# 48 instead of 40 tokens on fetched expert rows, with a fifth row block, six dot products moved into the gated units and three low parts moved to VectorE

## The reference

```
top_s, top_i = lax.top_k(s, PEER_TOPK)                       # per head and half key
best_s, best_pos = lax.top_k(cand_s, PEER_TOPK)
idx, gates = take_along_axis(cand_i, best_pos), softmax(best_s)
h   = gelu(einsum('chkd,cd->chk', peer_u[idx], x)) * gates   # 128 picks a token
out = einsum('chk,chkd->cd', h, peer_v[idx])
```

## Time and profile before

| | before |
|---|---|
| median of 3 runs | 968.71 us (968.62 to 969.97) |
| the profiled execution, its own time | 968.82 us |
| its span, first to last instruction | 967.0 us |
| busy: PE, PEld | 956.6 (99%), 918.7 (95%) us |
| busy: DVE, ACT, POOL | 741.6 (77%), 623.3 (64%), 589.8 (61%) us |
| granted TensorE clock over the span | 0.998 |

### The profile page before, as it was taken

The page is one execution under the profiler, slowest core; times in us unless marked ns, Lnnn a source line. Parts: engine busy times, 40 slices in busy tenths (PEclk is TensorE's granted clock), DMA queues, the critical chain, the costliest instruction groups (busy, mean ns, idle before and its releaser), DMA issues.

```text
span 967.0 us, 22095 instructions
## 1 busy us (share of the span) xinstructions
PE 956.6 (99%) x7344; PEld 918.7 (95%) x7344; DVE 741.6 (77%) x1606; ACT 623.3 (64%) x1227; POOL 589.8 (61%) x308
## 2 busy tenths in 40 slices
PE   9999999999999999999999999999999999999997
PEld 8998899999889999999999999999999999999996
DVE  7683673534756798888788888759888989898995
ACT  6773376555557666676899999865555555555553
POOL 4685624587425999989887888853434434343520
PEclk9999999999999999999999999999999999999999
DMA  7473313355654766666555456579999999999981
GB/s 263 143 235 125 131 48 110 110 175 187 224 181 152 233 221 215 215 215 215 188 177 182 175 195 217 197 277 395 338 370 340 362 356 348 357 343 356 354 296 44
DMA packets 64752, 223.96 MB, mean 232 GB/s; under 512 B 7964, under 2 KB 10012, under 8 KB 64573
## 3 DMA queue, kind: packets, MB, share of 16 engines
q1 hardware_dynamic: 52604, 180.54, 52.3%
q0 software_dynamic: 11520, 41.95, 12.3%
q10 hardware_dynamic: 576, 0.82, 0.2%
HBM read 221.28 MB, written 1.06 MB: 230 GB/s over the span
## 4 chain that ended last, share of the span: by engine, by line
PE 97%; DVE 1%; DMA 1%; ACT 0%; issue 0%; ACTq 0%; POOL 0%; DVEq 0%
PE PS L962 21%; PE PS L1034 20%; PE PS L966 12%; PE PS L1039 12%; PE PS L533 4%; PE PS L534 4%; PE PS L535 4%; PE PS L911 3%; PE PS L543 2%; PE PS L919 2%; PE PS L988 1%; PE PS L989 1%; PE PS L697 1%; PE PS L547 1%; PE PS L952 1%; PE PS L767 1%
## 5 line engine op out<-in xcount | busy, mean ns | idle before, releaser
L1566 POOL TENSOR_TENSOR lo<-raw,hi 128x1024 fp32r<-128x1024 f32 x191 | 456.9, 2410 | 143.3 <-ACT hi L1117 128.8
L1117 ACT CAST hi<-raw 128x1024 fp32r<-128x1024 f32 x203 | 212.6, 1048 | 48.8 <-DMA raw<-in_u_units 27.5
L962 PE MATMUL PS<-xb,hi 128*128 128x432 f32 x1024 | 225.1, 361 | 0.0
L1034 PE MATMUL PS<-xb,hi 128*128 128x432 f32 x1008 | 219.7, 359 | 0.0
L962 PEld LDWEIGHTS PS<-xb,hi 128*128 128x128 f32 x1024 | 182.8, 189 | 5.1
L1034 PEld LDWEIGHTS PS<-xb,hi 128*128 128x128 f32 x1008 | 179.7, 189 | 5.4
L2258 DVE TENSOR_TENSOR lo<-raw,hi 128x2048 fp32r<-128x2048 f32 x63 | 144.2, 2289 | 15.6 <-ACT hi L1456 12.2
L1456 ACT CAST hi<-raw 128x1024 fp32r<-128x1024 f32 x128 | 134.1, 1047 | 4.4 <-DMA raw<-in_v_units 4.3
L966 PEld LDWEIGHTS PS<-xb,lo 128*128 128x128 f32 x1024 | 133.6, 191 | 2.0 <-POOL lo L1566 0.6
L1039 PEld LDWEIGHTS PS<-xb,lo 128*128 128x128 f32 x1008 | 132.5, 191 | 2.8 <-DVE lo L2258 1.1
L1495 ACT CAST xb<-arena 128x216 fp32r (+1 forms) x126 | 47.0, 373 | 135.2 <-PE PS L1039 134.1
(11 more groups left out here) (361 smaller groups left out, 1536.1 us busy)
## 6 DMA issues: line engine op xcount, KB each, us to landing
raw<-in_u_units SPq DMA_DIRECT2D x128, 512.0 KB
raw<-in_v_units SPq DMA_DIRECT2D x128, 512.0 KB
raw<-in_w_in_units SPq DMA_DIRECT2D x43, 512.0 KB
raw<-in_w_q_units SPq DMA_DIRECT2D x16, 512.0 KB
raw<-in_w_proj_units SPq DMA_DIRECT2D x8, 512.0 KB
raw<-in_w_out_units SPq DMA_DIRECT2D x8, 512.0 KB
arena<-bias_rows SPq DMA_DIRECT2D x2, 512.0 KB, 4.8
arena<-in_subkeys_t SPq DMA_DIRECT2D x1, 1024.0 KB, 6.1
```

The costliest lines, as they stand in the source:

```text
L962: mm(o[:, 0:2 * TD].rearrange("p (s t) -> p s t", s=2), hi[:, w, P * k:P * k + P], xb[:, k, :, 0:TD], start=(k == 0), stop=False, skip_gro ...
L1034: return mm(PS[:, V_BANKS[c], 0:2 * TD].rearrange("p (s t) -> p s t", s=2), hi[:, (U_V + j) % 4, P * c:P * c + P], coef_slot(u + j)[:, :, ...
L1117: nc.scalar.copy(hi[:, j, :], raw[:, j, :]).then_inc(hi_made, 1)
L1566: nc.gpsimd.tensor_tensor(lo[:, w, :], raw[:, w, :], hi[:, w, :].bitcast(F32), ALU.subtract).then_inc(lo_pool, 1)
```

## The change

TG rises from 40 to 48 (GROUPS 32 and 16), so TD falls to 208, SECOND to 52, and there are 48 + 48 fetches instead of 40 + 40. A fifth row block is added (block 5 of the arena; SLOTS = 5). Eleven fetches instead of four are issued by GpSimd among the expert units, behind the low parts listed in GATHER_AT. Six dot products are done in the gated steps of EARLY_STEPS, behind the one-hots, and in every gated step the one-hots now come before second_halves and gated. The low parts of units 12, 28 and 44 are made by VectorE, behind expert_halves of the unit two before; GpSimd waits for each and passes the count on. Loops that held these steps are written out.

```diff
-GROUPS = [32, 8]
+GROUPS = [32, 16]
 TG = sum(GROUPS)
 TD = T - TG
 SECOND = TD // 4
...
-        rows_at = [area(P * TD + D * n, D) for n in range(4)]
+        rows_at = [area(P * TD + D * n, D) for n in ROW_BLOCKS]
...
+        rows_in = [sem(f"gathered_rows_in{n}") for n in range(SLOTS)]
...
-            LO_DVE_V = LO_FIRST + 2 * HEADS - LO_QUERY - (U_V + 2)
+            LO_DVE_V = LO_FIRST + 2 * HEADS - LO_QUERY + len(LO_BY_VECTOR) - (U_V + 2)
...
-            with pool.Fori(0, GATHER_AT) as i:
-                for j in range(4):
-                    make_lo(U_U, i, j)
-            pool.wait_ge(picks_in, PICKS_IN)
-            for g in range(4):
-                make_lo(U_U, GATHER_AT + g, 0)
-                gather(g)
-                for j in range(1, 4):
-                    make_lo(U_U, GATHER_AT + g, j)
-            with pool.Fori(GATHER_AT + 4, NKEYS // 4) as i:
-                for j in range(4):
-                    make_lo(U_U, i, j)
+                    out=rows_at[g % SLOTS], out_offset=None, in_=rows,
+                    in_offset=bass.IndirectOffsetOnAxis(ap=pick_row[:, n:n + 1], axis=0)).then_inc(rows_in[g % SLOTS], 16)
+
+            for u in range(NKEYS):
+                if u in LO_BY_VECTOR:
+                    pool.wait_ge(lo_dve, LO_FIRST + 2 * HEADS - LO_QUERY + LO_BY_VECTOR.index(u) + 1)
+                    pool.wait_ge(lo_pool, U_Q - LO_FIRST + LO_QUERY + u)
+                    pool.sem_inc(lo_pool, 1)
+                else:
+                    make_lo(U_U, u // 4, u % 4)
+                if u == GATHER_AT[0]:
+                    pool.wait_ge(picks_in, PICKS_IN)
+                if u in GATHER_AT:
+                    g = GATHER_AT.index(u)
+                    if g >= SLOTS:
+                        pool.wait_ge(rows_used, g + 1 - SLOTS)
+                    gather(g)
             make_lo(U_V, 0, 0)
             make_lo(U_V, 0, 1)
-            for g in range(4, 2 * GATHERS):
-                pool.wait_ge(rows_used, g - 3)
+            for g in range(len(GATHER_AT), 2 * GATHERS):
+                pool.wait_ge(rows_used, g + 1 - SLOTS)
                 gather(g)
...
                     columns_done[0] -= RANK_PER_UNIT
                     expert_halves(summed[0] // 4, summed[0] % 4)
+                    if summed[0] + 2 in LO_BY_VECTOR:
+                        make_lo(U_U, (summed[0] + 2) // 4, (summed[0] + 2) % 4)
                     summed[0] += 1
...
-                dve.wait_ge(rows_in[g % 4], 16 * (g // 4) + 16)
-                V.scalar_tensor_tensor(out=rows_at[g % 4], in0=rows_at[g % 4], scalar=1.0, in1=repeated[group], op0=ALU.mult,
+                dve.wait_ge(rows_in[g % SLOTS], 16 * (g // SLOTS) + 16)
+                V.scalar_tensor_tensor(out=rows_at[g % SLOTS], in0=rows_at[g % SLOTS], scalar=1.0, in1=repeated[group], op0=ALU.mult,
                                        op1=ALU.mult, accum_out=pick_dot[:, n:n + 1]).then_inc(rows_used, 1)
 
-            def gated_step(i, j):
-
-                gates_in(i, j)
+            def gated_step(i, j, early_dot=None):
+
+                n = 4 * i + j
+                if n < SECOND:
+                    gates_in(i, j)
+                if n + 2 < SECOND:
+                    one_hots(i, j + 2)
+                if early_dot is not None:
+                    dot(early_dot)
                 second_halves(i, j)
-                gated(i, j - 1, 4)
-                one_hots(i, j + 2)
+                gated(i, j - 1, min(4, SECOND + 3 - n))
...
             final = GATED_UNITS // 4 - 1
-            with dve.Fori(1, final - 1) as i:
-                for j in range(4):
-                    gated_step(i, j)
-            for j in range(4):
-                n = 4 * final - 4 + j
-                if n < SECOND:
-                    gates_in(final - 1, j)
-                second_halves(final - 1, j)
-                gated(final - 1, j - 1, min(4, SECOND + 3 - n))
-                if n + 2 < SECOND:
-                    one_hots(final - 1, j + 2)
+            for n in range(4, 4 * final):
+                if n == (EARLY_STEPS + [4 * final - 1])[0]:
+                    dve.wait_ge(picks_in, PICKS_IN)
+                gated_step(n // 4, n % 4, EARLY_STEPS.index(n) if n in EARLY_STEPS else None)
...
-            dve.wait_ge(picks_in, PICKS_IN)
-            g = 0
+            g = len(EARLY_STEPS)
             for q in range(1, NKEYS // 2):
                 value_operands(q // 4, q % 4)
                 while g < min(2 * GATHERS, ROWS_AFTER[q]):
@@ -2308,10 +2307,15 @@
...
-SPREAD_AT, GATHER_AT = 16, 26
+SPREAD_AT = 16
+LO_BY_VECTOR = [12, 28, 44]
+SLOTS, ROW_BLOCKS = 5, [0, 1, 2, 3, 5]
+EARLY_STEPS = [14, 19, 24, 29, 34, 39]
+GATHER_AT = [79, 84, 89, 94, 99, 104, 110, 112, 114, 116, 118]
 ROW_WORK = [(True, GROUPS[0] + n) for n in range(GROUPS[1])] + [(True, n) for n in range(GROUPS[0])]
 ROW_WORK += [(False, GROUPS[0] + n) for n in range(GROUPS[1])] + [(False, n) for n in range(GROUPS[0])]
-ROWS_AFTER = [len(ROW_WORK) * q // (NKEYS // 2 - 3) for q in range(NKEYS // 2)]
+EARLY = len(EARLY_STEPS)
+ROWS_AFTER = [EARLY + (len(ROW_WORK) - EARLY) * q // (NKEYS // 2 - 3) for q in range(NKEYS // 2)]
```

More of the change, by code:

```diff
@@ L304, in block_program @@
         act_evac = sem("act_evacuated")
-        dve_evac = sem("dve_evacuated")
         dve_step = sem("dve_step")
-        pe_step = sem("pe_step")
         act_step = sem("act_step")
@@ L359, in block_program @@
         staged_made, picks_in = sem("gathered_picks_staged"), sem("picks_and_rows_repeated")
-        rows_in = [sem(f"gathered_rows_in{n}") for n in range(4)]
+        rows_in = [sem(f"gathered_rows_in{n}") for n in range(SLOTS)]
         rows_used, dots_gelu, taker_made = sem("gathered_rows_used"), sem("gathered_dots_gelu"), sem("taker_made")
@@ L1478, in _ @@
             final = GATED_UNITS // 4 - 1
-            with act.Fori(1, final - 1) as i:
+            with act.Fori(1, final - 2) as i:
                 for j in range(4):
@@ L1483, in _ @@
                     low_one_hots(i, j + 1)
-            for j in range(4):
-                second_right_copy(final - 1, j)
-                second_half_gelu(final - 1, j - 1)
-                if 4 * final - 4 + j + 1 < SECOND:
-                    low_one_hots(final - 1, j + 1)
+            for n in range(4 * final - 8, 4 * final):
+                second_right_copy(n // 4, n % 4)
+                second_half_gelu(n // 4, n % 4 - 1)
+                if n + 1 < SECOND:
+                    low_one_hots(n // 4, n % 4 + 1)
             early_dots, late_dots = COLUMNS[1], COLUMNS[0]
@@ L1607, in gather @@
                 nc.gpsimd.indirect_dma_start(
-                    out=rows_at[g % 4], out_offset=None, in_=rows,
-                    in_offset=bass.IndirectOffsetOnAxis(ap=pick_row[:, n:n + 1], axis=0)).then_inc(rows_in[g % 4], 16)
-            with pool.Fori(0, GATHER_AT) as i:
-                for j in range(4):
-                    make_lo(U_U, i, j)
-            pool.wait_ge(picks_in, PICKS_IN)
-            for g in range(4):
-                make_lo(U_U, GATHER_AT + g, 0)
-                gather(g)
-                for j in range(1, 4):
-                    make_lo(U_U, GATHER_AT + g, j)
-            with pool.Fori(GATHER_AT + 4, NKEYS // 4) as i:
-                for j in range(4):
-                    make_lo(U_U, i, j)
+                    out=rows_at[g % SLOTS], out_offset=None, in_=rows,
[14 more added lines that the diff above has]
+                    gather(g)
             make_lo(U_V, 0, 0)
             make_lo(U_V, 0, 1)
-            for g in range(4, 2 * GATHERS):
-                pool.wait_ge(rows_used, g - 3)
+            for g in range(len(GATHER_AT), 2 * GATHERS):
+                pool.wait_ge(rows_used, g + 1 - SLOTS)
                 gather(g)
@@ L2240, in row_added @@
                 sums = row_sums[0 if n < GROUPS[0] else 1]
-                dve.wait_ge(rows_in[g % 4], 16 * (g // 4) + 16)
+                dve.wait_ge(rows_in[g % SLOTS], 16 * (g // SLOTS) + 16)
                 if n in (0, GROUPS[0]):
-                    V.tensor_scalar(sums, rows_at[g % 4], pick_coef[:, n:n + 1], None, ALU.mult).then_inc(rows_used, 1)
+                    V.tensor_scalar(sums, rows_at[g % SLOTS], pick_coef[:, n:n + 1], None, ALU.mult).then_inc(rows_used, 1)
                     return
                 dve.wait_ge(rows_used, g)
-                V.scalar_tensor_tensor(out=sums, in0=rows_at[g % 4], scalar=pick_coef[:, n:n + 1], in1=sums, op0=ALU.mult,
+                V.scalar_tensor_tensor(out=sums, in0=rows_at[g % SLOTS], scalar=pick_coef[:, n:n + 1], in1=sums, op0=ALU.mult,
                                        op1=ALU.add).then_inc(rows_used, 1)
```

1 line of the change is left out of this document (removed).

## The result

The changed kernel takes 962.88 us (median of 12, 960.74 to 968.63), the kernel before 968.83 us (12 runs, 967.84 to 970.66): ratio 0.9948, 95% interval 0.993 to 0.9966. That is 6 us faster, where 12.3 were forecast. Three of the twelve executions took 967.9 to 968.6 us, at a mean granted clock of 0.994 to 0.996, the other nine at most 964.8 us at 0.997 to 0.999. The profiled execution took 964.81 us, its span is 963.0.

The account below looks back on a forecast made before the run. TensorE, busy 97% of the span, was taken as the bound. Gains of 14.8 us less 0.35, 1.4 and 0.7 gave 12.3, so 956.5 us from 968.8; range 952.0 to 965.0.

Parts of the forecast that it names:

- (a): Wide matmuls on TensorE: each loses 16 columns at 0.42 ns, 6.7 ns for each of 2048, 13.8 us gained.
- (b): Narrow matmuls on TensorE: losing 8 columns each gains 0, as a weight-load limit seems already reached; from above 6.9 us.
- The rival with 952.9 us: Narrow matmuls shrink too, at the slope between the two rows, gaining 3.6 us more; chance 0.14.
- (c): Gated units: SECOND falls from 54 to 52, so two units lose their one-hots, 1.0 us gained.
- The ranking: Expert units before the gated ones: VectorE, loaded with low parts, is late twice, costing 0.35 us at unit 28, 1.4 at 56.
- The wait at unit 28: TensorE waits there for the low part VectorE makes behind the halves of unit 26; cost 0.35 us, bounds 0 and 1.2.
- Dots among the gated units: Six gated steps: later halves delay ScalarE, so TensorE waits about 0.1 us each; cost 0.7 us, bounds 0 and 3.0.
- Fetches at nothing: Seven more fetches on GpSimd's queue among gated units, 0.96 us each, covered by its spare time; cost nothing.
- Value units: Stay bound by TensorE at 4.80 us a pair, VectorE at 97% of that, DMA at 380 GB/s without landing waits.
- Both DMA rivals: DMA bounds the value units: at 369 GB/s in all, 965.1 us, chance 0.13; at 358 GB/s, 974.2 us, chance 0.05.

Follow-up runs that it names:

- e12: Kernel before, wide matmuls after a unit's first cut to 424 columns among expert units, all to 416 among value units, products left out; 964.54 us, one run.
- e5: Changed kernel, wide matmuls after a unit's first cut to 384 columns among expert units, 400 among value units, products left out; 948.51 us, one run.
- e11: Changed kernel, wide matmuls after a unit's first cut to 408 columns among expert units, all to 384 among value units, products left out; 944.07 us, one run.
- e4: Changed kernel without the six early dot products, with the old step order and five early fetches instead of eleven; 962.81 us.
- e10: Changed kernel with line 2093 writing to PSUM and a copy back, and no low parts on VectorE; 959.87 us.
- e18: Changed kernel run again, unedited, in the last group of runs; 963.5 us.
- e6: Changed kernel with narrow matmuls over 128 of 208 columns, low products of 80 tokens left out; 961.32 us, one run.
- e1: Changed kernel run again, unedited, in the first group of runs; 962.05 us.
- e13: Changed kernel run again, unedited, in the fourth group of runs; 963.16 us.
- e3: Changed kernel with no low parts on VectorE, GpSimd making all those of the expert units; 962.49 us.
- e17: Changed kernel with line 2093 to PSUM, no low parts on VectorE, no early dots, old step order, five early fetches; 960.5 us.
- e9: Changed kernel with line 2093 writing to PSUM and a copy bringing it back; 961.43 us.
- e15: Changed kernel with line 2093 writing to PSUM and a copy back, measured once more in a later group; 962.65 us.
- e7: Changed kernel with the exponential and the transposes of the picks four units later (PICKS_AT 14 instead of 13); 968.51 us.
- e14: Changed kernel with the operation of line 2093 done three times over; 972.77 us.
- e2: Changed kernel's thinner matmuls alone: 40 fetched tokens, 8 tokens left out of the expert layer, none of the additions; 964.24 us.
- e8: Changed kernel with every fifth row block fetched twice, the second fetch behind the first; 1025.95 us.

## Why the prediction was right and wrong

Right: that it is faster, and the time lies in the range. The gain, 5.95 us, was just under half of the forecast. By its own steps:

- **(a), the step that failed: its size.** "each wide matmul loses 16 columns: 16 x 0.42 = 6.7 ns, 8 x 256 = 2048 of them, 13.8 us." The slope came from two widths 80 columns apart, and I used it for a step of 16. Measured, 3.9 ns each in place of 6.7: 76 dense units x 0.034 + 52 gated x 0.018 + 128 value units x 0.034 = 2.6 + 0.9 + 4.4 = 7.9 us. e12 has the same loss at 416 columns in the kernel before, so nothing that was added is to blame, and the value units of e5 and e11 have the full slope at 400 and 384. In the second pattern that e4, e10 and e18 show a dense unit is even longer than before's (2.487 against 2.447 us). Neither range nor rivals had a wide matmul that shrinks less than its columns; I had asked that of the narrow one only. In a gated unit the first wide matmul, behind the one-hots, gains 7 ns and the other seven 15, where a dense unit has 12 and 21. Why 416 lies above the line, and why a gated unit gains about half of what a dense one does, stays open.
- **(b) right.** Narrow part 0.88 us, and with narrow matmuls of 128 columns the unit stands too (e6). The rival with 952.9 us is refuted.
- **(c) right.** 2 x (2.965 - 2.447) = 1.04 us.
- **The ranking: mechanism right.** VectorE sets the date of unit 56. TensorE was to wait some 1.6 us there; beyond the 0.57 us of the transposes, units 55 and 56 are longer by 1.55 us in the first profile, 0.56 in e1 and 0.35 in the kernel before. Forecast: 1.75 us given back of 3.1 that TensorE gains to there. Measured from unit 0 to 58: TensorE gains 58 x 0.034 = 2.0 us, e1 is 1.0 us shorter than before, so 1.0 is given back; in the first profiled execution 144.64 us, all of it and 0.6 more. What share of it the three low parts have, the cause that I named, isn't shown: e13 and e18 take 145.6 and 145.7 us, e3 and e17, without the low parts, 143.8. VectorE's stay at line 2093, 1.56 us in e1 and 2.30 in the first profile, is in none of my steps although the kernel before has it too (2.31 us there); written to PSUM, the stretch takes 142.34 us in e9 but 143.69 in e15. With one profile each, and the changed kernel's own apart by 2.7 us, these don't rank the causes. The wait at unit 28 came as forecast, 0.35 us expected, 0.35 to 0.8 seen with unit 29's (e9, e1, first profile, e7), none in e4 and e18, whose TensorE was at the slow pace.
- **Dots among the gated units: too dear.** 0.7 us forecast, 0.1 measured (e1 against e4, one profile each).
- **Fetches at nothing: right on most, not on all.** Late landings by unit 101 cost 1.57 us in the first profile and 0.9 in e18's, 1.6 at unit 106 in e14's, none in e1, e3, e9, e10, e13 or e15. So e1's expectation was right for e1, that it is the hazard of one execution, but the place came back. e4 and e17, with five early fetches, show none. In these three profiles the fetch and the load beside it took 6.7 to 7.9 us to land, in e1 and e13 5.4 to 5.9; that they hold each other up is read from their times, not shown by a run.
- **Value units: right.** TensorE-bound, 377 GB/s (380 forecast). Both DMA rivals (965.1 and 974.2 us) are refuted by 2.416 us a unit at a share of 0.99. The Trainium skill's limit of about 358 GB/s for a core (DMA: Bandwidth & Descriptors, "Where 436 GB/s comes from") does not bind a core that runs alone: 387 GB/s over 200 us in e4.

Sum on e1's execution: 7.9 + 1.0 = 8.9 us less some 2.1 given back is the 6.8 measured (968.82 - 962.05); 14.8 and 2.45 had been forecast. Of the 2.1, 1.0 lie before unit 58, 0.4 before unit 0 and 0.7 between the last expert unit and the third value unit; for these two places the forecast had no term, and at the second the four profiles of the changed kernel differ by 0.9 us. So nearly all of the miss is term (a); that the given-back part comes out close is partly luck.

## What to carry to other kernels

A slope between two shapes is a mean over its step. Here a unit lay 20 to 30 ns above the line at some widths: a tenth of what 80 columns are worth, and nearly half of what 16 are. For a small step take neighbours of that very size, or give the term a low bound of its own. In a stage where VectorE sets the time, look for short VectorE operations whose duration is out of line with their neighbours and see whether they end with an operation of GpSimd: they are waits that the list of waits didn't show here, and writing to PSUM removed this one (0.30 us in e9). An addition that is there to protect against a shortage is worth its own run without it: here e17 has the whole gain without them, and lies 3 us below the kernel that has them and the waiting operation.

## What was not expected of the hardware

- Matmuls of 416 columns run at two steady paces at the same granted clock of 1.00: a wide part of 1.53 us or of 1.61 (every start 0.200 us after the last); the change from one to the other came within five units of a wait of TensorE, and the change back with one, but like waits in other profiles changed nothing. 384 columns showed two as well (units of 2.290 and 2.326 us, e5).
- Value units of 432, 416, 400 and 384 columns take 2.450, 2.416, 2.342 and 2.296 us: 16 columns are worth 34, 74 and 46 ns in turn.
- A VectorE operation of 0.3 us that needs what GpSimd holds was kept 7.31 us, past the ends of three of GpSimd's operations that followed without a pause (e2).
- TensorE had no work from 424.2 to 427.6 us in e2, and from 427.5 to 434.2 its granted clock was 0.53, all but the end at 1.2 GHz.
- A fetched row block lands 9.2 us after its issue (median of 38 in e8, at a DMA share of 0.85 to 0.97 for all but four).
